# A routed expert layer in 32-token blocks, with 32x32 transposes on VectorE and half of the next expert's first weights copied into place

## What is computed

```python
logits = xf @ router_w + router_b              # 1024 tokens, 32 experts
top_vals, top_idx = lax.top_k(logits, 4)
gates = softmax(top_vals)
# for every expert e, on the tokens that chose it:
h = xblk @ w1[e] + b1[e]                       # w1[e]: 1024 x 2048
g, u = split(h, 2);  g = min(g, 7);  u = clip(u, -7, 7)
act = g * sigmoid(1.702 * g) * (u + 1)
y[token] += gate * (act @ w2[e] + b2[e])       # w2[e]: 1024 x 1024
```

## Time and profile before

| | |
|---|---|
| median of 3 runs (lowest, highest) | 3151.4 us (3151.2, 3155.1) |
| the profiled execution: its time, its span | 3155.3 us, 3153.3 us |
| mean granted TensorE clock in it | 0.94 |
| TensorE matmul / VectorE / ScalarE / GpSimd busy | 90% / 22% / 12% / 9% |
| DMA | 504 MB, 160 GB/s over the span |
| the chain that ended last | TensorE 58%, DMA 11% |

### The profile page before, as it was taken

One profiled execution on the slowest core, in us unless ns is written; L12 is line 12 of the kernel. 1 busy time (PEld: TensorE's weight loads), 2 busy tenths in 40 slices (PEclk: granted clock), 3 DMA queues, 4 the chain that ended last, 5 costly groups with the idle time before them and its releaser, 6 DMA issues.

```text
span 3153.3 us, 32994 instructions
## 1 busy us (share of the span) xinstructions
PE 2825.6 (90%) x12166; PEld 1171.7 (37%) x12167; DVE 707.0 (22%) x1741; ACT 392.8 (12%) x824; POOL 278.8 (9%) x367
## 2 busy tenths in 40 slices
PE   8999997999989679899999799899799979975575
PEld 4645565444445223233333233233233323321121
DVE  4334776011133211111111111111111111110012
ACT  2002553000013000000000000000000000000002
POOL 0000000000001211011111011011111111110000
PEclk9998898999999789899999899899899989987787
DMA  3100002200053586513553737553866664487773
GB/s 128 53 27 0 1 1 76 84 21 25 9 185 119 195 320 221 192 27 132 180 190 87 290 90 279 201 184 129 338 233 213 242 250 163 150 330 307 303 291 127
DMA packets 139364, 504.08 MB, mean 160 GB/s; under 512 B 26912, under 2 KB 44704, under 8 KB 106304
## 3 DMA queue, kind: packets, MB, share of 16 engines
q1 hardware_dynamic: 106176, 460.22, 37.8%
q0 software_dynamic: 19536, 43.10, 6.6%
q10 hardware_dynamic: 13600, 0.10, 0.2%
HBM read 469.06 MB, written 34.64 MB: 160 GB/s over the span
## 4 chain that ended last, share of the span: by engine, by line
PE 58%; DMA 11%; SPq 1%; DVE 1%; issue 1%; POOL 0%; DVEq 0%; ACT 0%; ACTq 0%; POOLq 0%
PE xbank L1252 32%; PE xbank L1275 18%; DMA w_hi<-in_w 9%; PE xbank L1206 3%; PE xbank L1242 1%; PE xbank L1262 1%; PE xbank L1234 1%; DMA reg_r<-in_w 1%; PE xbank L1269 1%; PE xbank L1192 0%; SPq L860 0%; DVE reg_h L1168 0%; DMA w_hi<-in_b 0%; POOL slot_rows L884 0%; SPq L856 0%
## 5 line engine op out<-in xcount | busy, mean ns | idle before, releaser
L1252 PE MATMUL xbank<-reg_r,stage 128*64 128x512 f32 x2592 | 597.0, 615 | 197.0 <-DMA reg_r<-in_w 196.3
L1252 PE MATMUL xbank<-w_hi,stage 128*64 128x512 f32 x2592 | 572.5, 593 | 9.6 <-DMA w_hi<-in_w 9.6
L1275 PE MATMUL xbank<-reg_r,stage 128*64 128x512 f32 x2592 | 572.4, 594 | 2.4 <-DVE stage L1149 2.4
L1252 PEld LDWEIGHTS xbank<-reg_r,stage 128*64 128x64 f32 x2592 | 190.9, 142 | 591.3 <-issue 586.1
L1275 PEld LDWEIGHTS xbank<-reg_r,stage 128*64 128x64 f32 x2592 | 182.6, 137 | 363.6 <-issue 354.7
L1252 PEld LDWEIGHTS xbank<-w_hi,stage 128*64 128x64 f32 x2592 | 181.0, 137 | 355.2 <-issue 319.7
L531 PE MATMUL pair<-reg_r,reg_h 128*128 128x512 f32 (+1 forms) x640 | 252.7, 550 | 0.3 <-DMA reg_r<-in_w_in 0.3
L1149 DVE COPY stage<-xbank 128x512 f32<-128x512 f32 x81 | 56.0, 691 | 792.6 <-PE xbank L1242 788.3
L1138 DVE TENSOR_SCALAR stage<-xbank 128x512 f32<-128x512 f32 x81 | 56.0, 692 | 620.3 <-PE xbank L1252 620.3
L902 POOL TENSOR_TENSOR idxs<-idxa,tok 128x1 int32<-128x1 int32 x81 | 15.2, 188 | 1677.2 <-ACT stage L979 1677.2
L531 PEld LDWEIGHTS pair<-reg_r,reg_h 128*128 128x128 f32 x640 | 119.2, 191 | 114.2 <-issue 110.1
(11 more groups left out here) (187 smaller groups left out, 2031.4 us busy)
## 6 DMA issues: line engine op xcount, KB each, us to landing
reg_r<-in_w SPq DMA_DIRECT2D x64, 2048.0 KB, 12.6
w_hi<-in_w SPq DMA_DIRECT2D x64, 2048.0 KB
reg_r<-in_w SPq DMA_DIRECT2D x128, 1024.0 KB, 7.3
reg_r<-in_w_in SPq DMA_DIRECT2D x4, 2048.0 KB, 7.8
reg_r<-in_x SPq DMA_DIRECT2D x8, 512.0 KB, 3.5
reg_ka<-in_w_in SPq DMA_DIRECT2D x8, 512.0 KB, 3.9
reg_g<-in_w_in SPq DMA_DIRECT2D x8, 512.0 KB, 3.9
reg_r<-in_w_o SPq DMA_DIRECT2D x1, 4096.0 KB, 17.0
```

Source lines behind the costliest of these rows:

```text
L1252: ins = pe.matmul(up_bank[b][h][QB * c:QB * c + QB, :], xT[b][:, k % HG, QB * (k // HG):QB * (k // HG) + QB], w1k[k][:, h * FF + c * FG:h ...
L1275: ins = pe.matmul(y_bank[b][QB * j:QB * j + QB, 0:DG], actT[:, k % HG, QB * (k // HG):QB * (k // HG) + QB], w2r[:, k, j * DG:(j + 1) * DG] ...
```

## The change

- **Blocks of 32 tokens** (`QB` = 32, `NG` = 4): four groups of 256 features, four column groups of 32 in `up` and `down`. `up` does both halves h in one matmul of 512 columns, `down` works on 256 columns. Scratch tiles are 256 wide instead of 512.
- **Transposes on VectorE**, block by block of 32x32 (`turn_x`, and at the end of `swiglu`). TensorE's transposes and their two stores go. So that such a transpose fits, slice k of w1 is now made of rows j*256 + k*32 + q (j = 0..3, q = 0..31), where it was 128 rows in sequence. w2 is cut in the same way, with two rows side by side.
- **A spare region** `next_lo` = `reg_r[:, 16384:]` receives k 0 to 3 of the next expert's w1. In every block VectorE's `refill` copies these four slices (128x2048 each) to their place: from `next_lo` at the first block of an expert, otherwise from themselves onto themselves (the slot number in `listi[.,3,.]` is 2 or 0).
- **Loads**: eight transfers of 1 MB for w1 instead of four of 2 MB, four of 1 MB for w2. SP's order for each expert is k 4 to 7 of the next, `next_lo` 0 of the one after, w2 of the next, `next_lo` 1 to 3.
- The slot list of a block is fetched in four parts (`load_slots`), not two.

```diff
-QB = 64
-NPAD = 104
+QB = 32
+NPAD = 168
...
-W1P, W2P = 4, 4
+W1P, W2P = 8, 4
...
+        next_lo = reg_r[:, 16384:].rearrange("p (k n) -> p k n", k=4)
+        lo_from = reg_r[:, :].rearrange("p (s k n) -> p s k n", s=3, k=4)
...
-        w1_d = a["w1"][0].rearrange("e (q k p) n -> e q p k n", p=P, k=2)
-        w2_d = a["w2"][0].rearrange("e (q k p) n -> e q p k n", p=P, k=2)
+        w1_d = a["w1"][0].rearrange("e (j k q) n -> e k j q n", j=NG, q=QB)
+        w2_d = a["w2"][0].rearrange("e (j h q k) n -> e h j q (k n)", j=NG, h=W2P, q=QB)
...
             for q in range(W2P):
-                sp.dma_start(w2r[:, 2 * q:2 * q + 2, :], w2_d[0, q]).then_inc(w2_in[q], 16)
+                sp.dma_start(w2q[q], w2_d[0, q]).then_inc(w2_in[q], 16)
+            for k in range(4):
+                sp.wait_ge(w1_in[k], 16)
+                sp.dma_start(next_lo[:, k, :], w1_d[1, k]).then_inc(w1_in[k], 16)
...
+            def load_hi(i, ended):
+                for k in range(4, KD):
+                    sp.wait_ge(w1_used[k], ended)
+                    sp.dma_start(w1k[k], w1_d[bass.ds(i + 1, 1), k].rearrange("o j q n -> (o j) q n")).then_inc(w1_in[k], 16)
...
+            def load_next_lo(i, ended, k):
+                sp.wait_ge(w1_filled[k], ended)
+                sp.dma_start(next_lo[:, k, :], w1_d[bass.ds(i + 2, 1), k].rearrange("o j q n -> (o j) q n")).then_inc(w1_in[k], 16)
+            with sp.Fori(0, NEXP - 2) as i:
+                ended = sp.value_load(listi[0:1, 2, bass.ds(i, 1)], min_val=1, max_val=NBLOCKS)
+                load_hi(i, ended)
+                load_next_lo(i, ended, 0)
+                load_w2(i, ended)
+                for k in range(1, 4):
+                    load_next_lo(i, ended, k)
...
-                dve.tensor_tensor(act_s, ul, sg, ALU.mult).then_inc(act_ready, 1)
...
+                dve.transpose(actT[b], act_s).then_inc(act_ready, 1)
+
+            def refill(n):
+
+                loaded = dve.value_load(listi[0:1, 0, bass.ds(n, 1)], min_val=16, max_val=16 * NEXP)
+                slot = dve.value_load(listi[0:1, 3, bass.ds(n, 1)], min_val=0, max_val=2)
+                for k in range(4):
+                    dve.wait_ge(w1_used[k], n)
+                    dve.wait_ge(w1_in[k], loaded)
+                    dve.sem_inc(refill_go, 1)
+                    dve.tensor_copy(w1k[k], lo_from[:, bass.ds(slot, 1), k, :].rearrange("p o n -> p (o n)")).then_inc(w1_filled[k], 1)
...
+                        refill(n + 1)
                         swiglu(n, 1 - m)
+                        turn_x(n + 2, 1 - m, i + (m + 1))
                         dve.wait_ge(y_done, n)
                         choose(n + 1, m)
...
+                    for c in range(NG):
+                        ins = pe.matmul(up_bank[b][QB * c:QB * c + QB, :].rearrange("p (h f) -> p h f", h=2),
+                                        xT[b][:, QB * k:QB * k + QB],
+                                        w1k[k].rearrange("p (h f) -> p h f", h=2)[:, :, c * FG:(c + 1) * FG],
+                                        start=(k == 0), stop=(k == KD - 1))
+                    ins.then_inc(w1_used[k], 1)
```

More of the change, by code:

```diff
@@ L725, in expert_half @@
         w1k = [w1_half[k // 4][:, k % 4, :] for k in range(KD)]
-        w1q = [w1_half[q // 2][:, 2 * (q % 2):2 * (q % 2) + 2, :] for q in range(W1P)]
         w2r = reg_r[:, 8192:16384].rearrange("p (k n) -> p k n", k=KD)
+        next_lo = reg_r[:, 16384:].rearrange("p (k n) -> p k n", k=4)
+        lo_from = reg_r[:, :].rearrange("p (s k n) -> p s k n", s=3, k=4)
+        w2q = [reg_r[:, 8192 + q * 2 * D:8192 + (q + 1) * 2 * D] for q in range(W2P)]
         stage = sb("stage", [P, 6 * D])
@@ L745, in expert_half @@
         e_all = sb("e_all", [96, NPAD])
[L746 to L747 removed]
+        listf = sb("listf", [P, 4, NPAD])
+        listi = sb("listi", [P, 4, NPAD], I32)
         iters_i = sb("iters_i", [P, 1], I32)
@@ new lines, in _ @@
+            with sp.Fori(0, NEXP - 2) as i:
[5 more added lines that the diff above has]
+                    load_next_lo(i, ended, k)
+            ended = sp.value_load(listi[0:1, 2, NEXP - 2:NEXP - 1], min_val=1, max_val=NBLOCKS)
+            for k in range(4, KD):
+                sp.wait_ge(w1_used[k], ended)
+                sp.dma_start(w1k[k], w1_d[NEXP - 1, k]).then_inc(w1_in[k], 16)
@@ L864, in _ @@
+            for q in range(W2P):
+                sp.wait_ge(w2_used[q], ended)
+                sp.dma_start(w2q[q], w2_d[NEXP - 1, q]).then_inc(w2_in[q], 16)
             n_iters = block_iters(sp)
@@ L956, in load_slots @@
                 if not (isinstance(half, int) and half == 0):
-                    act.wait_ge(idx_in[b], half * (16 * NG))
+                    act.wait_ge(idx_in[b], half * 64)
                 row = act.value_load(listi[0:1, 1, bass.ds(n, 1)], min_val=0, max_val=TABROWS - QB)
@@ L1245, in up @@
-            def up(b, loaded, ks):
-                for k in ks:
-                    if k % 2 == 0:
-                        pe.wait_ge(w1_in[k // 2], loaded)
-                    for h in range(2):
-                        for c in range(NG):
-                            ins = pe.matmul(up_bank[b][h][QB * c:QB * c + QB, :], xT[b][:, k % HG, QB * (k // HG):QB * (k // HG) + QB],
-                                            w1k[k][:, h * FF + c * FG:h * FF + (c + 1) * FG], start=(k == 0), stop=(k == KD - 1))
-                    if k % 2 == 1:
-                        ins.then_inc(w1_used[k // 2], 1)
+            def up(n, b, loaded, ks):
+                for k in ks:
+                    if k < 4 and not isinstance(n, int):
+                        pe.wait_ge(w1_filled[k], n)
+                    else:
+                        pe.wait_ge(w1_in[k], loaded)
+                    for c in range(NG):
[4 more added lines that the diff above has]
+                    ins.then_inc(w1_used[k], 1)
@@ L1257, in up_bias @@
             def up_bias(n, b):
                 pe.wait_ge(sel_ready, n + 1)
-                for h in range(2):
-                    for c in range(NG):
-                        pe.matmul(up_bank[b][h][QB * c:QB * c + QB, :], sel[b][:, :],
-                                  b1p[:, h * FF + c * FG:h * FF + (c + 1) * FG], start=False, stop=False)
+                for c in range(NG):
+                    pe.matmul(up_bank[b][QB * c:QB * c + QB, :].rearrange("p (h f) -> p h f", h=2), sel[b][:, :],
+                              b1p[:, :].rearrange("p (h f) -> p h f", h=2)[:, :, c * FG:(c + 1) * FG], start=False, stop=False)
```

102 lines of the change are left out of this document (43 added, 59 removed).

## The result

| | before | changed |
|---|---|---|
| median (lowest, highest), 4 runs each | 3153.3 us (3151.2, 3156.4) | 5465.3 us (5454.9, 5474.0) |
| span of the profiled execution | 3153.3 us | 5460.7 us |
| mean granted TensorE clock | 0.94 | 0.72 |

The changed kernel takes 1.733 times as long, 95% interval 1.729 to 1.737. The forecast was 5420 us.

What follows compares the result with a forecast made beforehand. Weight loads on four DMA engines were taken to bound the changed kernel: 1045 start + 3722 slices + 444 idle + 135 sharing + 40 + 32 = 5418 us of span, rounded to 5420 us for the median; range 5150 to 6050.

Steps and rivals of the forecast that it cites:

- The step that decided: Weight loads: transfers are cut by outermost source entries, so four groups leave four engines working and 12 idle.
- the queue starts at: Routing: w2 of the first expert issued 22 us later than 1023.4, first norm some 30 us later; start at 1045.
- slices and what shares the engines: Weight queue: 376 slices at 9.9 us are 3722 us, plus 135 us for gathers and scatters on the same engines.
- the queue idle: Weight queue idles 12(b - 5) us for an expert of b blocks; ten experts, 37 blocks above five, 444 us.
- behind the last slice: End of kernel: three blocks and a rest, 40 us, then 32 us from last matmul to end.
- A slice: One 1 MB weight transfer: 9.9 us on four engines at 26.5 GB/s each, against 2.5 us on 16.
- TensorE's part: Block of 32 tokens: four groups side by side, `up` 7.0 us, `down` 3.5, sum 11.1; 21.7 if only two.
- VectorE's part: Block: four copies at 1.22 us, transposes 0.42 each; about 8.5 us in all, 12.8 with copies at 2.29.
- GpSimd's chain: Scatter then gather: 11 us, block taken as 12; VectorE's port lock could add 75 to 110 us, left out.
- Rival 1: Weight loads: all 16 engines still share a slice, 2.5 us each, blocks decide; about 3030 us; chance 0.10.
- Rival 2: All 16 engines but slow block: TensorE groups two at a time, 4300 us, or copies at 2.29, 3150 to 3250; 0.05.
- Rival 3: Four engines and the slow block of 21.7 us: queue idle about 1050 us, total 6030 us; chance 0.05.

Runs made afterwards that it cites:

- run 1: Changed kernel with source patterns of w1 and w2 beginning with 16 groups of 8 rows instead of 4 of 32: 3728.7 us.
- run 2: Changed kernel with 8 groups of 16 rows in front in w1 and w2: 4540.9 us.
- run 4: Kernel before the change with only the source patterns of w1 and w2 made to begin with 4 groups: 6312.3 us.
- run 8: Changed kernel with 32 groups of 4 rows in front in w1 and w2: 3072.2 us.
- Run 10: Changed kernel, four groups in front, without the spare region and the copies: 6253.9 us.
- run 9: Run 5's kernel without the spare region and the copies: 3286.0 us, 1.042 of the kernel before.
- run 5: Changed kernel with each 1 MB slice one contiguous piece of HBM, 128 rows in front, token columns reordered to match: 3073.4 us, 0.974 of the kernel before.
- run 6: Changed kernel with 128 rows in front but spread in HBM, transposes reading and product writing in matching order: 3045.5 us.
- run 11: Changed kernel with only TensorE's three thresholds loaded afresh from memory for each pair of blocks, as in all the experiments: 5527.2 us.
- run 12: Run 6's kernel again, for its interval against the kernel before: 3050.9 us, 0.968 of it.
- run 7: Changed kernel with 16 groups of 8 rows in front, the groups' first rows side by side in HBM, rows inside a group far apart: 3737.9 us.

## Why the prediction was right, point by point

The step that decided held: a slice whose source begins with four groups goes to four engines (share 0.26, 107 GB/s), whatever else is long in it. Runs 1, 2, 4 and 8 agree with the rule on the number of engines that the prediction cites from the Trainium skill (DMA: Bandwidth & Descriptors, "Why a DMA increments its semaphore by 16 and not by 1"): shares near 1.0, 0.5, 0.25, and 1.0 again for 32 groups. The terms of the sum, against the packets of 8 KB in the trace of the changed kernel (376 slices from 1067.8 to 5393.4 us, w2 of the first expert in front; idle is a time without any such packet):

| term | forecast | measured |
|---|---|---|
| the queue starts at | 1045 | 1068 |
| slices and what shares the engines | 3722 + 135 = 3857 | 3900 |
| the queue idle | 444 | 426, in 12 gaps |
| behind the last slice | 40 + 32 = 72 | 67 |
| span | 5418 | 5461 |

- **A slice.** 9.9 us forecast. Undisturbed ones take 9.7 to 9.8 us in the trace, packets 309 to 311 ns; with gathers, scatters and gaps between transfers the mean is 10.4 (3900 us over 376 slices). The two terms together were 43 us too small.
- **The idle queue.** The form 12(b - 5) held, its size partly by luck. The forecast miscounted: by the list of blocks eleven experts have six or more, and they have 38 blocks above five, not ten with 37. At 12 us that is 456 us, and the forecast would have been 5430. The trace has exactly eleven gaps for the eleven experts, from 10.8 us (6 blocks) to 142.4 (18 blocks), 420 us in all, so 11.05 us for each of the 38 blocks, where the block itself took 10.65 to 11.3. The twelfth gap is one of 5.7 us near the end. Against those 420 us the miscount made the term 12 us too small and the block of 12 us made it 36 too large. Run 10 tells how far such working can be trusted: its total was 54 us off, but the trace has 1059 us of gaps where I had 1270, and 4058 us of slices where the changed kernel has 3900 and I had expected some 80 less.
- **The start.** The sign in routing came: the first norm starts at 943.7 where it was 908.6, 35 us later (some 30 forecast). I had w2 issued 22 us later; it was 31 (1054.8 against 1023.4). I had counted the loads that hold the engines, not that SyncE itself is held while it issues them (16.46 and 11.08 us). And its first packet came 13 us behind the issue, which the forecast had as nothing (in run 8 it is 12 us). Together the queue started 23 us late; the second half of the first w1 was done at 1051.4, and no weight packet ran for 16.3 us.
- **TensorE's part.** 11.1 us forecast, 10.65 measured. `up` halves took 3.64 us each (I had 3.5 for each of the two), `down` 3.67 (3.5).
- **VectorE's part.** The copy took 1228 ns, the 1.22 of the cast's row; the transposes 446 and 424 ns (0.42). The product that writes in the transposes' order (L1163) took 621 ns where I had 421, which nothing waits for here.
- **GpSimd's chain.** I kept the lock out of the sum at 75 to 110 us. It exists (2.3 us a block, run 9 against run 5), but doesn't show in the block's time of 10.65 to 11.3 us: rows are gathered too early for it to matter. I had left it out because no row showed it, which was not the reason.
- **The rivals.** Rival 1 gave about 3030 us if all 16 engines shared a slice. Runs 5, 6 and 8 are that case: 3073, 3046 and 3072. Some 60 to 90 of those are the thresholds (run 11); TensorE's waits at a change of expert are in run 12's rows above, 35 us for the upper half, 36 for w2 and 80 for the copies. Rivals 2 and 3 needed TensorE's groups two at a time or a copy of 2.29 us; the timeline and the 1228 ns rule out both.

The larger misses came in the experiments. I took "all 16 engines busy" for "full rate" and had 2880 to 3000 us for run 1; they were busy at half the rate. Then I blamed addresses, and runs 6 and 7 refuted it from both sides.

## What to carry to other kernels

Read the source pattern of every large transfer from its front: the outermost count sets how many engines work on it, and the page shows it at once as a DMA share that stays near a quarter or a half while others wait for data. A share near 1.00 isn't yet full rate: divide GB/s by the share and by 16. Here that gives 24 to 26 GB/s per engine with 4, 32 or 128 entries in front and 14 with 16; where it comes out low, group the rows otherwise. When a new layout of tokens asks for such a pattern, look for a permutation of the rows inside the contraction that keeps 128 in front: here a stride in a transpose gave it (the transpose L1183 went from 424 to 629 ns, which TensorE didn't wait for), and turned 73% slower into 3% faster.

## What the runs showed of the hardware that I had not expected

- A transfer to 128 partitions with exactly 16 entries in front at the source moves 229 GB/s on 16 busy engines; with 32 or 128 it moves 383 to 405 (the same 20 us of the program). At 8 entries, slices of one kernel take 309 to some 585 ns a packet on average, drifting from one to the other over ten slices or more.
- SyncE is held at the issue when several transfers go to few engines: 16.46 us for four of 1 MB on four engines (16.23 in run 4, for w2), 11.08 us for the small one behind them; four on eight engines took 3.99 (run 2) and four on sixteen 2.55 (run 8). Few engines alone aren't enough: two of 2 MB on four engines were issued in 2.01 us (run 4).
- Three register loads from memory, in place of two and one carried over, leave a gap of up to 1.6 us on TensorE at the head of a pair of blocks; with them the changed kernel takes 62 us (1.1%) more (run 11).
- VectorE's float32 copies of 2048 lengthen GpSimd's mean operation from 0.74 to 1.78 us (index), 1.59 to 2.52 (scatter) and 1.00 to 1.31 (gather): run 5 against run 9.
